# A two-layer hybrid decoder trunk on eight cores: the opening norm staged as a pipeline, the value fold placed between output-projection tiles, the other norms in timed pieces, attention products three steps behind

## What is computed

```python
h = layer_norm(x, ln_in_g, ln_in_b)
for l in range(DEPTH):                      # 2
    mix = hybrid_mixer(h, ...)              # 8 MLA, 4 NSA and 4 MoBA heads, one in- and one out-projection
    h = layer_norm(ALPHA * h + mix, ln1_g[l], ln1_b[l])
    h = layer_norm(ALPHA * h + memory_cross_attention(h, mem, wq, wkv, wo), ln2_g[l], ln2_b[l])
    h = layer_norm(ALPHA * h + squared_relu_mlp(h, w1, w2), ln3_g[l], ln3_b[l])   # hidden 8192
```

## Time and profile before

| | |
|---|---|
| median of 3 runs | 7944.08 us (7892.37 to 8165.55) |
| the profiled execution | 7899.35 us |
| its span, slowest core (core 3) | 7897.9 us |
| spans of the eight cores | 7862.3 to 7897.9 us |
| PE busy | 7046.6 us (89%) |
| DVE busy | 2857.2 us (36%) |
| ScalarE busy | 1965.3 us (25%) |
| DMA | 725.62 MB, mean 92 GB/s |

### The profile page before, as it was taken

How to read it: one execution, slowest core, us unless ns; L and a number is a source line. 1 busy time by engine, 2 the same in 40 slices (tenths; PEclk the granted TensorE clock), 3 DMA queues, 4 the chain that set the end, 5 groups by cost and what they waited for, 6 DMA issues and landing times.

```text
span 7897.9 us, 92856 instructions; the slowest of 8 cores (7862.3 to 7897.9 us)
## 1 busy us (share of the span) xinstructions
PE 7046.6 (89%) x40308; PEld 3509.2 (44%) x40308; DVE 2857.2 (36%) x6051; ACT 1965.3 (25%) x2717; POOL 227.2 (3%) x434
## 2 busy tenths in 40 slices
PE   3499876799999999999989987769999999999997
PEld 1244554354444444444444455435444444444443
DVE  3244561135642223222233546212555222242224
ACT  3311443354330001100031144335424000110001
POOL 0000000000000000000000000000000000000000
PEclk8799988899989999999999998889999999999999
DMA  4321226444374444644441112643437444464443
GB/s 139 106 45 25 43 48 120 81 117 152 115 192 75 77 78 96 127 76 75 77 111 37 40 26 49 126 83 80 156 112 213 86 75 76 76 149 79 75 75 85
DMA packets 147881, 725.62 MB, mean 92 GB/s; under 512 B 21840, under 2 KB 52816, under 8 KB 79376
## 3 DMA queue, kind: packets, MB, share of 16 engines
q0 software_dynamic: 61920, 396.65, 28.9%
q1 hardware_dynamic: 85552, 323.02, 12.0%
HBM read 976.78 MB, written 135.27 MB: 141 GB/s over the span
## 4 chain that ended last, share of the span: by engine, by line
PE 78%; DVE 10%; DMA 6%; ACT 5%; issue 1%; SPq 0%; DVEq 0%; ACTq 0%; POOLq 0%
PE ps L509 77%; DVE b_y L531 2%; ACT ps L516 2%; DVE b_ym L531 2%; DMA fa<-b_fst 2%; PE ps L513 1%; DVE b_x L531 1%; DMA fb<-b_fst 1%; DMA b_x<-x 1%; ACT b_P L516 1%; ACT b_ln_hb L516 1%; DMA b_memT<-memt 0%; DMA b_wup<-up 0%; DMA b_rtab<-rope 0%; DMA b_w2s<-w 0%
## 5 line engine op out<-in xcount | busy, mean ns | idle before, releaser
L509 PE MATMUL ps<-b_w2s,b_Hb 128*128 128x512 bf16 x8192 | 1789.1, 380 | 93.0 <-DVE b_ym L531 61.2
L509 PE MATMUL ps<-b_hT,b_w1s 128*128 128x512 bf16 x8192 | 1788.1, 381 | 6.9 <-DMA b_w1s<-w 3.5
L509 PEld LDWEIGHTS ps<-b_w2s,b_Hb 128*128 128x128 bf16 x8192 | 801.0, 98 | 1070.6 <-DVE b_ym L531 73.2
L509 PEld LDWEIGHTS ps<-b_hT,b_w1s 128*128 128x128 bf16 x8192 | 804.5, 98 | 982.9 <-issue 35.9
L516 ACT ACTIVATE b_rr<-ps 128x1024 bf16<-128x1024 f32 x256 | 262.1, 1024 | 3040.9 <-PE ps L509 3040.9
L524 DVE TENSOR_TENSOR b_ym<-b_ym,ps 128x512 f32<-128x512 f32 x768 | 519.4, 687 | 781.2 <-PE ps L509 781.2
L516 ACT ACTIVATE b_P<-ps 128x1024 bf16<-128x1024 f32 (+4 forms) x784 | 658.4, 855 | 428.2 <-PE ps L509 423.1
L524 DVE TENSOR_TENSOR b_Hb<-b_rr 128x1024 bf16<-128x1024 bf16 x256 | 177.2, 692 | 1606.3 <-ACT b_rr L516 1606.3
L509 PE MATMUL ps<-b_wout,b_hT 128*128 128x512 bf16 x2048 | 447.1, 379 | 0.2 <-DVE b_y L531 0.2
L513 PE MATMUL ps<-b_ident,b_ln_hb 128*128 128x128 bf16 x1568 | 120.6, 239 | 240.5 <-ACT b_ln_hb L516 239.6
L509 PEld LDWEIGHTS ps<-b_wout,b_hT 128*128 128x128 bf16 x2048 | 199.1, 98 | 235.0 <-DVE b_y L531 0.7
(11 more groups left out here) (383 smaller groups left out, 7426.0 us busy)
## 6 DMA issues: line engine op xcount, KB each, us to landing
b_w1s<-w POOLq DMA_DIRECT2D x128, 1024.0 KB, 8.1
b_w2s<-w POOLq DMA_DIRECT2D x128, 1024.0 KB, 8.0
b_y<-hres SPq DMA_DIRECT2D x64, 1024.0 KB, 8.3
hres<-b_y SPq DMA_DIRECT2D x64, 1024.0 KB, 5.1
b_fw<-wkv POOLq DMA_DIRECT2D x64, 512.0 KB, 7.3
b_ym<-hres SPq DMA_DIRECT2D x32, 1024.0 KB, 16.1
b_x<-x SPq DMA_DIRECT2D x16, 1024.0 KB, 5.9
hres<-b_x SPq DMA_DIRECT2D x16, 1024.0 KB, 4.0
```

What stands on the lines that cost most here:

```text
L509: return S.op("pe", lambda e: e.matmul(out, lhsT, rhs, start=start, stop=stop, skip_group_check=True), reads=reads, writes=writes)
```

## The change

- **Opening.** The norm is split into methods (`square`, `norm`, `norm2`, `cast`, `trans`), and `ln_in(t, half)` issues, around tile t's two products, the transposes of tile t+2, the cast of t+3, the sums of t+5 and the norm of t+4. Five `x` buffers; the memory tokens are tiles 16 and 17 of the same pipeline. `x` is loaded first; `wiA` waits until the bias row has landed, `wiB` until the third `x` tile has, `wiC` is issued at tile 8.
- **Other norms.** `Slots` counts nanoseconds of TensorE work in place of groups. Squares are taken after every second column group and written to SBUF; `norm` is due 1500 after the tile's last group, `norm2` 3000, `cast` 8000 and `trans` 12500 later, and two tiles' norms are at least 8000 (8200) apart. A row buffer is reused once its tile is marked free, if need be by issuing pieces early (`slots.until`). Transposes of norms have banks 6 and 7; products rotate over six banks (`nb` modulo 6).
- **Fold.** All 32 key-side units first (16 in NSA, 16 in the first MLA pair), then 32 value-side units between the column groups of the output projection, from its second tile on. Evacuation is by ScalarE in NSA and the output projection, by DVE in MLA. The up-projection's evacuation in MLA moves from ScalarE to DVE.
- **Attention.** PV lags three steps; five `P` buffers. In MoBA and NSA value products have banks 4 to 6 and filler shares bank 7 with the transposes; in MLA filler has 6 and 7. NSA's compressed step handles two heads at once with fewer DVE calls; NSA's output is copied by one ScalarE call in place of four DVE calls.
- **Smaller.** `compress` copies keys and values with ScalarE to a layout that PE reads without a stride; `rms_job` transposes two tiles later, with three buffers.
- **MLP.** `l2` takes single banks; the last chunk does its first four tiles with the column group outside, then four tiles one by one.

```diff
     def nb(n):
-        p = (bpos[0] + n - 1) // n * n % 8
-        bpos[0] = (p + n) % 8
+        p = (bpos[0] + n - 1) // n * n % 6
+        bpos[0] = (p + n) % 6
...
+        def go(self, t, y, after=None):
+            w = max(slots.now + 1500, self.next)
+            self.next = w + self.space
+            slots.at(w, lambda: self.norm(t, y, st))
+            slots.at(w + 3000, lambda: self.norm2(t, y, st))
+            if self.hT is not None:
+                slots.at(w + 8000, lambda: self.cast(t, y, st))
...
+                slots.at(w + 12500, lambda: self.trans(t, st))
...
-                src = kcs if i == 0 else vcs
-                v3 = src[:, :].rearrange("p (n s) -> p n s", s=16)
+                raw = kcs if i == 0 else vcs
+                src = A.alloc("cs", [128, 16, 128], BF16, A_KR if i == 0 else A_MQ)
+                act(src[:, :, :], raw[:, :].rearrange("p (n s) -> p s n", s=16), AF.Copy, raw.tks, [src.tk])
...
-            if 0 <= i - 2 < n:
-                steps[i - 2].PV(live.pop(i - 2), lambda lag, fn: late.append((i + lag, fn)))
+            if 0 <= i - 3 < n:
+                steps[i - 3].PV(live.pop(i - 3), lambda lag, fn: late.append((i + lag, fn)))
...
-    orot = Rot([4, 5])
-    FB, MB = 6, 7
+    orot = Rot([4, 5, 6])
+    frot = Rot([7])
+    MB = 7
...
-                    fill.add(fold.gen(28))
-                    tot += 28 * 8 * 216
...
+                    fill.add(fold.gen(32 - fold.u))
+                    tot += (32 - fold.u) * 8 * 216.0
...
-                rest = 64 - fold.u
-                for _ in fold.gen(rest):
-                    pass
...
+        fold.place(169728, 133120, [A_KR, 126976, 177920, 182016], [131072], "act", lambda: nb(1))
+        fill.add(fold.gen(32))
+        per = 32 * 1728.0 / 46
+
+        def between(t, c):
+            if t > 0:
+                fill.run(per)
...
-                for t in range(8):
-                    b = nb(4)
-                    if t == 0:
...
+                for c in range(4):
+                    if c == 0:
+                        bs = [nb(1) for _ in range(4)]
```

More of the change, by code:

```diff
@@ new lines, in norm2 @@
+        def norm2(self, t, y, st):
+            sd, sdk = st["sd"]
+            rstd, rk = sm()
+            S.op("dve", lambda e: e.reciprocal(rstd, sd), reads=sdk, writes=rk)
+            stt(y[:, :], y[:, :], rstd, self.b[:, :], ALU.mult, ALU.add, [y.tk, self.b.tk] + rk, [y.tk])
+            dk = [self.dst_tk[t]] if self.dst_tk is not None else []
+            S.dma("sp", self.dst[t * 128:(t + 1) * 128, :], y[:, :], reads=[y.tk], writes=dk)
+            if self.hT is None:
+                st["free"] = True
@@ new lines, in cast, with trans @@
+        def cast(self, t, y, st):
+            st["hb"] = self.hb.next()
+            act(st["hb"][:, :], y[:, :], AF.Copy, [y.tk], [st["hb"].tk])
+            st["free"] = True
+        def trans(self, t, st):
+            p = self.trbank()
+            for j in range(16):
+                tp(bkb(p + j // 8, (j % 8) * 128, (j % 8 + 1) * 128), st["hb"][:, j * 128:(j + 1) * 128],
+                   [st["hb"].tk], [bank[p + j // 8]])
+            for g2 in range(2):
+                cp(self.evac, self.hT[:, g2 * 8:(g2 + 1) * 8, t * 128:(t + 1) * 128],
+                   bkb(p + g2).rearrange("p (j q) -> p j q", j=8), [bank[p + g2]], [self.hT.tks[t]])
+            st["done"] = True
@@ new lines, in gen @@
+                if i < 4:
+                    b = self.fbank()
+                    for kt in range(16):
+                        mm(bk(b, 0, 256), w[:, kt, :], self.memT[:, kt, :], kt == 0, kt == 15, [w.tk, self.memT.tk], [bank[b]])
+                    cp(self.evac, kv[:, i, :], bk(b, 0, 256), [bank[b]], [kv.tk])
+                    self.u += 1
+                    self.load(last)
+                    yield 1728
+                    continue
+                st = self.sts.next()
+                q = i - 4
@@ L1123, in gen @@
+                for hf in range(2):
+                    b = self.fbank()
+                    if side == 0:
                         first = True
@@ L1229, in moba_extra @@
             return f
-        catt_chunk(12), catt_chunk(13), catt_chunk(14), catt_chunk(15)
+        for kt in range(12, 16):
+            catt_chunk(kt)
         steps = []
@@ L1480, in attention @@
                 load_wout(3, PBs + 16384)
[L1481 to L1490 removed]
+            run_attn(steps, Ps, lambda i, n: tot / (n - 4))
+            fill.drain()
             cur = nxt
[L1492 removed]
+        orot.bufs[:] = [4, 5, 6]
+        frot.bufs[:] = [7]
+        orot.i = frot.i = 0
+        return wo_slabs, fold
     R0 = 186112
@@ new lines, in ln_norm, with ln_cast, ln_tr, ln_in @@
+    def ln_norm(v):
+        if v < NT + 2:
+            sts[v] = {}
+            if v < NT:
+                ln0.norm(v, xs[v], sts[v])
+                ln0.norm2(v, xs[v], sts[v])
+    def ln_cast(v):
+        if v < NT + 2:
+            ln0.cast(v, xs.pop(v), sts[v])
+            ldx(v + 5)
+    def ln_tr(v):
+        if v < NT:
+            ln0.trans(v, sts[v])
+        elif v < NT + 2:
+            mem_trans(v - NT, sts[v])
+    def ln_in(t, half):
+        if t is None:
+            for u in range(-5, 0):
+                if u + 5 < NT:
+                    ln_stats(u + 5)
+                if u + 4 >= 0:
+                    ln_norm(u + 4)
+                if u + 3 >= 0:
+                    ln_cast(u + 3)
+                if u + 2 >= 0:
+                    ln_tr(u + 2)
+        elif half == 0:
+            ln_tr(t + 2)
+        else:
+            ln_cast(t + 3)
+            if t + 5 < NT:
+                ln_stats(t + 5)
+            ln_norm(t + 4)
@@ L1804, in build_program @@
         if not last:
+            slots.until(lambda: all(tails[t]["free"] for t in (8, 9)))
             wA = load_in(l + 1, "A", A_S1)
+            slots.until(lambda: all(tails[t]["free"] for t in (10, 11)))
             wB = load_in(l + 1, "B", A_S2)
+            slots.until(lambda: tails[12]["free"])
     slots.flush()
```

609 lines of the change are left out of this document (292 added, 317 removed).

## The result

| | before | after |
|---|---|---|
| fastest runs, us | 7892, 7944 | 7356, 7358, 7374 |
| profiled execution, us | 7899 | 7358 |
| span of its slowest core, us | 7897.9 | 7356.3 |
| PE busy, share of the span | 89% | 93% |

The ratio is 0.930, with a 95% interval of 0.922 to 0.938: 7.0% faster, some 540 us. The median of after's runs is 7366; the forecast was 7220, so 146 us too low, above the likeliest case's own range (7130 to 7300) and inside the wide one.

A forecast was written before the change was run, and what follows sets the result against it. It took PE, busy 89% of the span, as the bound, with six loose places where PE waits or its clock falls short. Terms summed to -678 us from 7899, giving 7221, said as 7220; likeliest case 7130 to 7300, overall 7100 to 7390.

The forecast's parts named there:

- the MLP's: MLP's last chunks, next openings and the kernel's end: -84 us, bounds -130 and -30.
- Table and compress: Rotary table's hole after the opening shrinks by half, -8 us; unstrided compress products in the input projection, -13.
- the opening: Kernel's start: overlapping tiles run at the busiest engine's pace, 8.2 us a turn; 370 us becomes 173, taken as -195.
- the cross-attention's output: Norm stage there: early squares and a later reciprocal end DVE's waits, -24 us a layer, -48 in all.
- MLA with the fold: First MLA pair and the fold's tail: tail gone, fewer waits, -359 us over both layers.
- the output projection: Takes 32 fold units of 1.8 us that PE cannot hide, plus waits: +126 us for both layers.
- Three banks, two heads per DVE call and copies moved to ScalarE (busy 119 of 252) should end most of the 40: NSA: waits of 23.7 us for two banks and 16.2 for DVE's copies mostly end; -45 us a layer, -90.
- attention keeps its waits: Rival: shared bank 7 loses NSA's 90 us and the pairs' 20; 7330 us, chance 0.10.
- norms tied: Rival: cross-attention's output and MLP's last chunks gain nothing from norms counted in product columns; 7352 us, chance 0.08.
- fold twice: Rival: value units' stores in the output projection hold ScalarE and what follows; 295 us at worst, 7365 us, chance 0.12.
- the 3.4 us ahead of the next block stay: MLP, after a last chunk: the 3.4 us stay, since the next block's slabs are still requested when the chunk's are done.
- The slower one: Rival: MLP's second product on single banks lets PE's clock drop; 8060 us at 47% of products, 9006 with all, chance 0.02.

The follow-up runs named there:

- e8: Changed kernel with the fold's 32 value units in a row behind the first MLA pair, none in the output projection, copies on DVE; mean span 7475 us, 141 more.
- e10: e5 plus residual loads one norm later, norms 5.5 us apart behind the second block, slab B behind five x tiles; 7278 and 7307 us.
- e5: Changed kernel with exponential ahead of filler, MoBA filler bank 6, paired selection transposes in NSA, three residual tiles requested early; mean span 7273 us, 61 less.
- e1: Changed kernel with the attention step's exponential issued ahead of the filler; NSA 241.0 to 223.6 us, mean span 7306 us, 28 less.
- e7: Changed kernel with value products lagging two steps in place of three; MoBA 154.9 and 152.8 us (+11, +10), four cores 7374 to 7406 us.
- e3: Changed kernel with filler alone in bank 6 and products in banks 4 and 5 in MoBA and NSA; MoBA 133.9 us, NSA 252.4.
- e11: e10 with the first block's last chunk running tiles 4 to 7 column group outside, each slab freed behind its group; slowest cores 7254 to 7267 us.

## Why the prediction was wrong, and where right

The median came out 146 us above the forecast, outside the likeliest case's own range, though inside the wide one. By stages the sum missed by 128 us (-678 against -550). NSA's term is 71 of them and the MLP's 42: these are the two steps that failed. Table and compress missed by 14, the opening and MoBA by 13 each, the cross-attention's output by 4; MLA with the fold, the output projection and rms gave 29 more than forecast, which hides part of the miss.

**Right: the direction, and the three largest terms in their order.** Opening, MLA with the fold, and output projection were to give -428; they gave -440. e8 shows the reason as argued: a unit waits where PE has only the fold, and is covered where 16 products stand between.

*Opening.* The pace was right and the start wrong. The first product came at 48 us (45 in the sum). Eight turns from the fourth on took 63 us, 7.9 each, against 8.2, and the last three 6.2 each, against 6.6. But the fourth turn began at 87 us, where the sum has it at 75 (50 + 3 x 8.2):

```profile
82.24 1.89 PE L511 MATMUL ps<-b_ident,b_ln_hb 128*128 128x128 bf16 x16 [7.43 <-ACT b_ln_hb L514]
...
86.64 3.61 PE L507 MATMUL ps<-b_wiA,b_hT 128*128 128x512 bf16 x16
```

From 31.5 us until then DMA is at 1.01 and 0.85 of its engines' time, and DVE waits 18 us for x. Two later turns, whose casts came late, took 20 us in place of 13. Which load goes first changed nothing (e10), so the rate of the transfers is the likely bound, which was not tried by itself. Start and late turns together are the 13 us, and some that the other turns gave back.

**Wrong: the step "Three banks, two heads per DVE call and copies moved to ScalarE (busy 119 of 252) should end most of the 40".** It priced NSA at -45 a layer; measured -12 and -7. It treated the two waits as a matter of banks and of DVE's load. (1) DVE's load fell as said, 157 to 124 us, but the selection's wait did not: it is a chain of dependent small calls with one copy between two transposes of one bank. With both transposes side by side, one copy, and a step more of time it is 5 us (e5); which of these did it was not taken apart. (2) The copies were costed by ScalarE's idle time (busy 119 of 252 us). What counts in a queue is place: a copy that waits for products of PE holds the exponential behind it, and PE's scores wait for that. I had asked this question of the output projection's stores, and not here. e1 gives 17 us a layer back, e5 25 in layer 1, of the 33 and 38 that were missing. (3) MoBA at 0 took the lag's gain and the bank's cost as two terms that cancel. They are not independent: the lag is worth 10 us where the filler shares the bank (e7), and hides part of what the sharing costs; with a bank of its own the stage is only 2 us below the kernel before (e3). In sum the stage lost 7. The rival *attention keeps its waits* named the bank as the cause; that holds in MoBA, while in NSA the third bank is a gain and the order on ScalarE was the largest loss found. The time alone does not choose between the rivals: 7352 (norms tied) and 7365 (fold twice) lie nearer to the measured 7356 to 7374 than this rival's 7330, but the stages speak against both (below).

**Wrong: "the 3.4 us ahead of the next block stay", and nothing queued behind the norms that slide.** The four MLP ends themselves gave -73 against -84: last chunk with the chunk behind it -15 and -25, the stretch to `wiC` -17, the kernel's end -16 (87 us, as forecast). What I left out is SP. Held norms hold their stores, and the stores hold the eight residual loads, which go out 20 to 30 us later in their stage than before: 11 us in the first chunks that add residuals of the two layers and 8 in the second block of layer 1. Another 8 come with the transposes of two more tiles that slid there from the cross-attention's output (57.0 to 62 and 60.4 us in the first chunk of `Hb`; on core 0 PE waits 2.4 us for one of their casts); the sum let about two norms slide out of that stage, and priced them at nothing in this one. e5 and e10 remove most of the first two. The slab wait grew from 3.4 to 7 us. The row of the changed kernel puts it down to a DVE call (`b_small`), that of e10 to the slab's DMA; e11, which frees the slabs earlier, ends it in layer 1, so it is the slab.

*Small terms.* The rotary table's hole did not shrink (15.7 to 17.9 us). The compress copy costs PE 3.4 us, not 2, and the products behind it take 3.6, not 2.1, in place of 7.5:

```profile
220.69 3.60 PE L507 MATMUL ps<-b_hT,b_wiC 128*128 128x512 bf16 x8 [17.87 <-DVE b_rt_1283 L522]
```

```profile
334.89 3.57 PE L507 MATMUL ps<-b_cs,b_cw_0_1643 128*128 128x127 bf16 x32 [3.40 <-ACT b_cs L514]
```

*The other rivals.* The fold does not pay twice: the output projection's stretch has PE busy 301 of 306 us. The norms are not tied: the cross-attention's output gave -44 of -48, and the MLP's four ends -73 of -84. The slower one did not come: in the MLP's body, with single banks over six, PE is busy 663 of 663 us at a granted clock of 1.00. The Trainium skill, "TensorE: Matmul & The Clock Gate", section "A second HAM failure mode: psum-queue depth-cycling", ties a swinging clock to brief idling between the groups of a kernel that goes through its banks. The row here shows the same going through banks without the idling, and no swing.

What stays open: NSA at 216 us still waits some 39 us on PE in e5; its parts (value products behind DVE 12.7, scores 9.4, memory tokens 5.4) were not taken apart. What holds SP on two cores in e10 was not tried.

## What to carry to other kernels

A call moved to an idle engine is priced by its place in that engine's queue: ask what it waits for, and what stands behind it. Filler costs least where the products around it cover its copies and stores: a unit cost 1.9 us between the projection's products and 4.2 in a row. When work is allowed to slide into the next stage, follow its stores: the next stage's loads stand behind them on the same queue.

## What the runs showed of the hardware

Four slabs of 1 MB requested within 7 us of each other, beside stores and residual loads of the same size, took 23.3 us to land (median), against 8.2 over the whole execution; the eight residual tiles requested in one burst took 29.7 (29.0 in the kernel before):

```profile
b_w1s<-w POOLq DMA_DIRECT2D x4, 1024.0 KB, 23.3
```

```profile
b_ym<-hres SPq DMA_DIRECT2D x8, 1024.0 KB, 29.7
```

A load into a buffer whose store had just been issued held SP until that store was done, and with it all that stood behind it in SP's queue: 92.2 us in eight waits between layer 1's blocks. DVE ended these norms at 6466.6 us, and the last of their stores was issued at 6490, the last load at 6504.
